# One matmul for both token halves: reversing the second half of the tokens in an HGRN2 recurrence

## The chip, the cores and the metric

The kernel runs on one core of a Trainium2 chip. The metric is the device time of one execution, in microseconds (us). Five engines work at once: TensorE (PE; its weight loads are shown as PEld), VectorE (DVE), ScalarE (ACT), GpSimd (POOL) and SyncE (SP), which here only issues DMAs. A profile is of one execution.

## The reference, cut to what matters

Two transformer blocks over 256 tokens of 2048 features, all in fp32. The change concerns one part of the first block, a gated linear recurrence with 8 heads of 128 by 128, taken along the tokens:

```python
log_f = log(lb + (1 - lb) * sigmoid(z)); k = (1 - lb) * sigmoid(-z); qf = silu(q) * 128 ** -0.5
b = cumsum(log_f)                       # along the tokens
# for every token t, over all s <= t:
scores[t, s] = sum_k q[t, k] * k[s, k] * exp(b[t, k] - b[s, k])
o[t] = sum_s scores[t, s] * v[s]
```

The rest of the model depends on the order of the tokens too, in three places: rotary angles and the sliding window of the first block's attention, the rotary angles of the second block's attention, and a Fourier transform along the tokens.

## The kernel before, in words

The program's main queue is a list of weight blocks (`plan`, line 85): each block is 256 tokens by 512 columns of some projection, cut into units of 256 weight rows. A unit is two times two times three fp32r matmuls of 512 columns, since each factor is split into a high and a low part (`unit`, line 900). ScalarE copies the high part of a weight tile (`high`, line 1293) and VectorE subtracts it to get the low part (`low`, line 1862); the four `raw` places, and more places in the arena in some stretches, are loaded by DMAs on SP's queue in the order of `ITEMS` (line 659).

Everything else is woven between the units by hand. `timetable` (line 372) gives each stage the slot at which it starts, and `drive` (line 635) lets every live stage take one step for each slot, on each engine's own queue: a `yield` is a step to the next slot. Engines meet through semaphores (`e.wait_ge`).

The recurrence is such a stage, `hgrn(b)`, for b = 0, 1, a group of four heads each; b = 1 starts two slots after b = 0. `QT`, `KT` and `BT` hold q, k and b with the features on the partitions and 256 token columns a head, the two halves of 128 (m = 0, 1) side by side. The scores of a token in the second half against one in the first half are "level 0" (L = 128). Within each half of 128, seven levels (L = 64 to 1) split every run of 2L tokens in two: the earlier L tokens are keys and the later L are queries, and the reference point of the decay is the last of the earlier ones, so that no exponent is positive. For a level,

1. VectorE writes two tensor_tensors of 512 elements into `E` (the differences of b), ScalarE takes `exp` of all 1024, and VectorE multiplies by k and q in place (lines 2083 to 2089);
2. TensorE multiplies. At level 0 these are four matmuls, one a head, with 128 columns (line 1042). At the others eight, one a head and half: the stationary operand is the 128 columns of `E` of that half, keys and queries alike, and the moving operand is the 64 query columns, taken in runs of L (line 1050);
3. VectorE copies the scores that count from PSUM into `s` with a mask (`copy_predicated`, lines 2102 to 2106), one instruction a level.

Four matmuls for the diagonal follow a group of two heads at a time (line 1059), then the products with v (line 1071). On TensorE a level is one slot in four, and each group of four heads has its own; the levels of b = 0 and b = 1 alternate.

`copy` and `f` on ScalarE (line 1281), `tt` on VectorE (line 1837) and `mm` on TensorE (line 864) are helpers, so that the profile shows their line for all their callers.

Of the kernel before, what the change touches and what calls it, by code (L numbers as in the profile page):

```python
# [15 lines left out]
P = 128  # L16
# [14 lines left out]
K_ID, K_U, K_ONE, K_AM, K_HM = 0, 128, 256, 384, 640  # L31
K_IF = K_HM + 64 * len(LEVELS)
K_MH = K_IF + 32
K_N = K_MH + 4


def constants():
    c = np.zeros((P, K_N), np.float32)
    i, j = np.arange(P)[:, None], np.arange(P)[None, :]
    c[:, K_ID:K_ID + P] = i == j  # L40
    c[:, K_U:K_U + P] = i <= j
    c[:, K_ONE:K_ONE + P] = 1.0
    c[:, K_AM:K_AM + P] = np.where(j > i, 0.0, -1e30)
    c[:, K_AM + P:K_AM + 2 * P] = np.where(j <= i, 0.0, -1e30)
# [8 lines left out]
    ang = 2.0 * np.pi * ((t[:, None] * t[None, :]) % 256) / 256.0  # L53
# [428 lines left out]
def program(nc, A, out):  # L482
    es = ExitStack()
    with es:
# [79 lines left out]
        QT, KT, BT = (kb(o, 8).rearrange("p (h t) -> p h t", h=8) for o in (0, 8, 16))  # L564
# [42 lines left out]
        def hg_s(b):  # L607
            return kb(72 + 4 * b, 4).rearrange("p (h m t) -> p h m t", h=4, m=2)
# [240 lines left out]
        def pe(e):  # L849
# [159 lines left out]
            def hf(b):  # L1009
                yield from range(5)  # L1010
                e.wait_ge(*S.a_hf.at(b, "ln"))
                for s in range(2):
                    bk = bank(("hf", b, "c", s), S.v_hf, b, "c", s)
                    for z in range(2):
                        for m in range(2):
                            t = mm(bk[:, z * 256 + m * P:z * 256 + (m + 1) * P],
                                   TA[:, m, (2 * s + z) * P:(2 * s + z + 1) * P], CST[:, K_U:K_U + P], True, True)
# [14 lines left out]
            def hgrn(b):  # L1032
                E, s, x = hg_e(b), hg_s(b), hg_x(b)
                for n, L in enumerate((128,) + LEVELS):
                    yield
                    yield
                    yield
                    e.wait_ge(*S.v_hgrn.at(b, n, "m"))
                    if n == 0:
                        bk = bank(("hg", b, n), S.a_hgrn, b, "x")  # L1040
                        for h in range(4):
                            t = mm(bk[:, h * P:(h + 1) * P], E[:, h * 256:h * 256 + P], E[:, h * 256 + P:(h + 1) * 256], True, True)
                    else:
# [9 lines left out]
                k_, q_ = KT[:, 4 * b:4 * b + 4, :], QT[:, 4 * b:4 * b + 4, :]  # L1053
                for g in range(2):
                    bk = bank(("hgd", b, g), S.v_hgrn, b, "d", g)
                    for h in range(2):
                        for m in range(2):
                            ms = slice(m * P, (m + 1) * P)
                            t = mm(bk[:, (h * 2 + m) * P:(h * 2 + m + 1) * P], k_[:, 2 * g + h, ms], q_[:, 2 * g + h, ms], True, True)
                    t.then_inc(*S.p_hgrn.up(b, "d", g))  # L1060
# [6 lines left out]
                for m in range(2):  # L1067
                    bk = bank(("hgo", b, m), S.a_hgrn, b, "o", m)
                    for h in range(4):
                        o, vs = bk[:, h * P:(h + 1) * P], slice((4 * b + h) * P, (4 * b + h + 1) * P)  # L1070
                        t = mm(o, s[:, h, m, :], V[:, m, vs], True, m == 0)
# [200 lines left out]
        def act(e):  # L1272
# [128 lines left out]
            def hf(b):  # L1401
# [17 lines left out]
                for s in range(2):  # L1419
                    e.wait_ge(*S.p_hf.at(b, "k", s))  # L1420
                    e.wait_ge(*S.a_tab.at(1, 1))
                    e.wait_ge(*S.d_lbw.at())
                    copy(KT[:, 4 * b + 2 * s:4 * b + 2 * s + 2, :].rearrange("p s t -> p (s t)"),
                         BANK[bank_of["hf", b, "k", s]][:, :]).then_inc(*S.a_hf.up(b, "k", s))
                    yield

            def hq(b):
# [6 lines left out]
                for s in range(2):  # L1434
                    e.wait_ge(*S.p_hq.at(b, s))
                    copy(QT[:, 4 * b + 2 * s:4 * b + 2 * s + 2, :].rearrange("p s t -> p (s t)"),
                         BANK[bank_of["hq", b, s]][:, :], scale=float(128 ** -0.5)).then_inc(*S.a_hq.up(b, s))
# [232 lines left out]
            def fourier(l):  # L1670
                yield
                for g in range(8):
# [6 lines left out]
                    copy(cu[:, 0, 1, :], ps[:, 0, P:0:-1])  # L1679
                    copy(cu[:, 1, 1, :], ps[:, 1, P:0:-1], scale=-1.0).then_inc(*S.a_four.up(l, g))  # L1680
# [152 lines left out]
        def dve(e):  # L1833
# [150 lines left out]
            def att(half):  # L1984
                s, pt = att_s(half), att_p(half)
                mx, nm, e1, sm, rs = (att_stat(half, k) for k in range(5))
                for kvb in range(2):
                    h0 = 4 * (2 * kvb + half)
                    for n in range(2):
# [8 lines left out]
                        k0 = K_AM if n else K_AM + P  # L1998
# [47 lines left out]
            def hf(b):  # L2046
# [11 lines left out]
                for s in range(2):  # L2058
                    e.wait_ge(*S.p_hf.at(b, "c", s))
                    i.tensor_copy(BT[:, 4 * b + 2 * s:4 * b + 2 * s + 2, :].rearrange("p s t -> p (s t)"),  # L2060
                                  BANK[bank_of["hf", b, "c", s]][:, :]).then_inc(*S.v_hf.up(b, "c", s))
                    yield

            def hgrn(b):
                E, s, x = hg_e(b), hg_s(b), hg_x(b)
                q_, k_, b_ = (z[:, 4 * b:4 * b + 4, :] for z in (QT, KT, BT))
# [4 lines left out]
                for n, L in enumerate((128,) + LEVELS):  # L2071
                    nb = 256 // (2 * L) * 4

                    def cut(z):
                        w = z.rearrange("p h t -> p (h t)").rearrange("p (n z l) -> p n z l", z=2, l=L)
                        return w[:, :, 0, :], w[:, :, 1, :]
                    ev = E.rearrange("p (n z l) -> p n z l", z=2, l=L)
                    el, er = ev[:, :, 0, :], ev[:, :, 1, :]
                    (bl, br), (ql, qr), (kl, kr) = cut(b_), cut(q_), cut(k_)
                    ref = bl[:, :, L - 1:L].to_broadcast([P, nb, L])  # L2080
                    if n:
                        e.wait_ge(*S.p_hgrn.at(b, n - 1))
                    tt(el, ref, bl, ALU.subtract)
                    z = i.tensor_copy(er, br) if L == 128 else tt(er, br, ref, ALU.subtract)
# [7 lines left out]
                    if n:  # L2092
# [3 lines left out]
                        so = s.rearrange("p h m t -> p (h m) t").rearrange("p g (n z l) -> p g n z l", z=2, l=L)  # L2096
                        mk = CST[:, K_HM + 64 * (n - 1):K_HM + 64 * n].bitcast(I32).rearrange("p (n l) -> p n l", l=L)
                        ps = BANK[bank_of["hg", b, n]][:, :].rearrange("p (g n l) -> p g n l", g=8, l=L)
# [11 lines left out]
                for g in range(2):  # L2110
                    e.wait_ge(*S.p_hgrn.at(b, "d", g))
                    i.copy_predicated(s[:, 2 * g:2 * g + 2, :, :].rearrange("p h m t -> p (h m) t"),
                                      IDN.bitcast(I32).unsqueeze(1).to_broadcast([P, 4, P]),
                                      BANK[bank_of["hgd", b, g]][:, :].rearrange("p (g t) -> p g t", g=4)).then_inc(*S.v_hgrn.up(b, "d", g))
                yield from range(5)
                O, sq = E.rearrange("p (m n) -> p m n", m=2), s.rearrange("p h m t -> p (h m t)")
# [455 lines left out]
```

## Time and profile before

| | us |
|---|---|
| median of three runs | 2276.31 (2273.92 to 2279.29) |
| profiled execution, its own time | 2276.56 |
| its span, first to last instruction | 2274.8 |
| TensorE busy in the span | 2231.7 (98%) |
| VectorE busy | 1508.9 (66%) |
| ScalarE busy | 1114.3 (49%) |
| GpSimd busy | 43.6 (2%) |

TensorE's granted clock is 0.997 of full speed in the mean. Busy shares are averages over all stages, and a busy TensorE counts overlapping matmuls as one stretch, so that the distance from one start to the next tells more than a matmul's duration.

### The profile page before, as it was taken

Reading aid. Unit: us, or ns where it says so; the run is one execution under the profiler, and the core shown is the slowest. Engines: PE = TensorE matmul, PEld = TensorE weight load, DVE = VectorE, ACT = ScalarE, POOL = GpSimd, SP = SyncE. Lnnn points to the kernel's source line nnn. Section 1 sums busy time; section 2 is a strip of 40 time slices with the busy share of each in tenths; the row PEclk is TensorE's granted clock in tenths of the full one; section 3 lists DMA queues with packets and bytes.
Section 4 is the critical chain, followed back from the end, with each engine's and each line's share of the span. In section 5 each row is a group of like instructions: output and inputs, shape, how many; then the busy total and the mean of one; then the engine's idle time right before and its main releaser. Section 6 shows DMA issues by size and latency. Waiting matters only on the chain.

```text
span 2274.8 us, 27239 instructions
## 1 busy us (share of the span) xinstructions
PE 2231.7 (98%) x10708; PEld 1863.6 (82%) x10708; DVE 1508.9 (66%) x1887; ACT 1114.3 (49%) x1546; POOL 43.6 (2%) x64
## 2 busy tenths in 40 slices
PE   9999999999999999999999999999999999999997
PEld 7788888888887888888888888787898887788886
DVE  6575467768877777777777778766355566545655
ACT  6475455444445444444443444565466454446552
POOL 1000000100000000000000000000000000000000
PEclk9999999999999999999999999999999999999999
DMA  7544654499796888888889888473454583555573
GB/s 263 170 131 126 190 173 146 131 342 318 250 330 232 296 289 297 304 302 292 296 299 304 296 292 297 153 239 93 139 173 146 160 271 90 164 149 158 149 234 117
DMA packets 233263, 500.65 MB, mean 220 GB/s; under 512 B 15872, under 2 KB 24992, under 8 KB 231984
## 3 DMA queue, kind: packets, MB, share of 16 engines
q1 hardware_dynamic: 229872, 484.11, 65.9%
q0 software_dynamic: 3264, 14.81, 1.8%
q8 instruction: 84, 1.38, 0.2%
q14 instruction: 43, 0.35, 0.0%
HBM read 496.74 MB, written 2.12 MB: 219 GB/s over the span
## 4 chain that ended last, share of the span: by engine, by line
PE 89%; DVE 5%; ACT 3%; issue 1%; DMA 1%; POOL 0%; SPq 0%; POOLq 0%; ACTq 0%; DVEq 0%
PE bank L864 86%; PE bank L867 3%; DVE wl L1837 2%; ACT wh L1281 1%; ACT arena L1281 1%; DMA raw<-in_w_in 1%; DVE arena L1844 1%; DVE arena L1840 1%; DVE arena L1837 1%; DVE arena L1845 0%; DMA raw<-in_w_ple_gate 0%; ACT hh L1281 0%; DVE hl L1837 0%; DVE al L1837 0%; ACT L1281 0%
## 5 line engine op out<-in xcount | busy, mean ns | idle before, releaser
L1281 ACT ACTIVATE wh<-raw 128x1024 fp32r<-128x1024 f32 (+2 forms) x493 | 512.6, 1042 | 665.6 <-PE bank L864 623.1
L1837 DVE TENSOR_TENSOR wl<-raw,wh 128x1024 fp32r<-128x1024 f32 (+2 forms) x493 | 590.6, 1200 | 331.8 <-ACT wh L1281 329.4
L864 PE MATMUL bank<-wh,hh 128*128 128x512 f32 (+1 forms) x1568 | 620.8, 397 | 11.6 <-DVE hl L1837 7.0
L864 PE MATMUL bank<-wh,hl 128*128 128x512 f32 (+1 forms) x1568 | 606.1, 387 | 0.0
L864 PE MATMUL bank<-wl,hh 128*128 128x512 f32 (+1 forms) x1568 | 604.7, 387 | 0.0
L864 PE MATMUL bank<-wh,ah 128*128 128x512 f32 (+1 forms) x1168 | 457.3, 392 | 4.3 <-ACT arena L1281 2.6
L864 PE MATMUL bank<-wh,al 128*128 128x512 f32 (+1 forms) x1168 | 451.1, 387 | 0.0
L864 PE MATMUL bank<-wl,ah 128*128 128x512 f32 (+1 forms) x1168 | 450.2, 386 | 0.0
L864 PEld LDWEIGHTS bank<-wh,hh 128*128 128x128 f32 x1568 | 294.6, 188 | 71.3 <-issue 12.2
L1281 ACT ACTIVATE wh<-arena 128x1024 fp32r<-128x1024 f32 x191 | 202.5, 1061 | 295.4 <-PE bank L864 292.0
L864 PEld LDWEIGHTS bank<-wh,hl 128*128 128x128 f32 x1568 | 294.6, 188 | 61.0
L864 PEld LDWEIGHTS bank<-wl,hh 128*128 128x128 f32 x1568 | 295.2, 188 | 55.3
L1837 DVE TENSOR_TENSOR wl<-arena,wh 128x1024 fp32r<-128x1024 f32 x191 | 233.4, 1223 | 97.6 <-ACT wh L1281 96.1
L864 PEld LDWEIGHTS bank<-wh,ah 128*128 128x128 f32 x1168 | 219.2, 188 | 47.0 <-ACT arena L1281 3.4
L864 PEld LDWEIGHTS bank<-wh,al 128*128 128x128 f32 x1168 | 219.2, 188 | 44.2
L864 PEld LDWEIGHTS bank<-wl,ah 128*128 128x128 f32 x1168 | 219.5, 188 | 41.5
L864 PE MATMUL bank<-arena 128*128 128x128 f32 (+6 forms) x944 | 148.2, 304 | 2.0 <-DVE arena L1837 2.0
L864 PEld LDWEIGHTS bank<-arena 128*128 128x128 f32 (+1 forms) x944 | 130.2, 191 | 16.1 <-issue 4.8
L1844 DVE SCALAR_TENSOR_TENSOR arena<-arena,cols 128x1024 f32<-128x1024 f32 x101 | 129.1, 1278 | 0.0
L867 PE MATMUL bank<-cst,arena 128*128 128x128 f32 (+1 forms) x752 | 112.1, 275 | 8.8 <-DVE arena L1837 3.1
L867 PEld LDWEIGHTS bank<-cst,arena 128*128 128x128 f32 (+1 forms) x752 | 91.9, 141 | 33.1 <-ACT arena L1281 4.7
L1837 DVE TENSOR_TENSOR arena<-arena 128x512 f32<-128x512 f32 (+6 forms) x192 | 95.5, 541 | 24.2 <-ACT arena L1281 23.5
(126 smaller groups left out, 1397.5 us busy)
## 6 DMA issues: line engine op xcount, KB each, us to landing
raw<-in_w_in SPq DMA_DIRECT2D x247, 512.0 KB, 3.8
arena<-in_w_ada SPq DMA_DIRECT2D x106, 512.0 KB, 5.1
arena<-in_w_gate_up SPq DMA_DIRECT2D x100, 512.0 KB, 5.2
raw<-in_w_ada SPq DMA_DIRECT2D x86, 512.0 KB, 4.9
raw<-in_w_out SPq DMA_DIRECT2D x77, 512.0 KB, 4.8
raw<-in_w_gate_up SPq DMA_DIRECT2D x76, 512.0 KB, 5.2
arena<-in_w_down SPq DMA_DIRECT2D x47, 512.0 KB, 5.5
raw<-in_w_down SPq DMA_DIRECT2D x41, 512.0 KB, 5.6
```

Of the source, the lines that this page charges most:

```text
L864: return i.matmul(o, l, x, start=start, stop=stop, skip_group_check=False)
L867: return i.transpose(o, x, idn)
L1281: return i.activation(o, x, fn, scale=scale, **k)
L1837: return i.tensor_tensor(o, a, b, op)
L1840: return i.tensor_scalar(o, a, s1, s2, op0) if op1 is None else i.tensor_scalar(o, a, s1, s2, op0, op1)
L1844: return i.scalar_tensor_tensor(out=o, in0=a, scalar=s, in1=b, op0=op0, op1=op1)
```

## The change

The tokens of the second half are kept in reverse order: token 255 is the first of that half and 128 the last (`TOKENS`). The inputs that run along the tokens are reordered outside the program, and the result is put back. Inside, the cumulative sum of that half uses a triangular matrix of the other side, the attention masks and the Fourier table are written for the new order, and the Fourier copies read forward.

In each run of 2L positions, the earlier tokens are now the first L positions in the first half and the last L in the second half. So the key positions of the two halves complement each other: for each head and level, the 64 key columns of the one half and the 64 of the other are gathered into 128 contiguous columns of `E`, and the 128 query columns into another 128. One matmul of 128 by 128 a head then holds the scores of both halves, each half in its own rows and columns; what would mix the halves is not copied. The masked copy of a level becomes two instructions, one for each half, with a mask that has one column for each run. `QT`, `KT`, `BT` and `s` are laid out with the half ahead of the head. The diff, cut:

```diff
+TOKENS = [*range(128), *range(255, 127, -1)]
...
+    c[:, K_U + P:K_U + 2 * P] = i >= j
...
     for n, L in enumerate(LEVELS):
-        for b in range(P // (2 * L)):
-            o = K_HM + 64 * n + b * L
-            c[2 * L * b:2 * L * b + L, o:o + L] = 1.0
+        for m in range(2):
+            for b in range(64 // L):
+                r = 2 * L * b + m * L
+                c[r:r + L, K_LV[n] + m * (64 // L) + b] = 1.0
...
-        QT, KT, BT = (kb(o, 8).rearrange("p (h t) -> p h t", h=8) for o in (0, 8, 16))
+        QT, KT, BT = (kb(o, 8).rearrange("p (b m h t) -> p b m h t", b=2, m=2, h=4) for o in (0, 8, 16))
...
+        def hg_at(off, m_step, L, l_size):
+            return bass.AP(tensor=AR[:, :].tensor, offset=off, ap=[[88 * 256, P], [m_step, 2], [2 * L, 256 // L], [1, l_size]])
+
+        def hg_cut(k, L):
+
+            o = 256 * k
+            return hg_at(o, 512 + L, L, L), hg_at(o + L, 512 - L, L, L), hg_at(o + L - 1, 513, L, 1)
...
                     e.wait_ge(*S.v_hgrn.at(b, n, "m"))
-                    if n == 0:
-                        bk = bank(("hg", b, n), S.a_hgrn, b, "x")
-                        for h in range(4):
-                            t = mm(bk[:, h * P:(h + 1) * P], E[:, h * 256:h * 256 + P], E[:, h * 256 + P:(h + 1) * 256], True, True)
-                    else:
-                        bk = bank(("hg", b, n), S.v_hgrn, b, n, "p")
-                        for h in range(4):
-                            for m in range(2):
-                                c0 = h * 256 + m * P
-                                rhs = E[:, c0:c0 + P].rearrange("p (n z l) -> p n z l", z=2, l=L)[:, :, 1, :]
-                                o = bk[:, (2 * h + m) * 64:(2 * h + m + 1) * 64].rearrange("p (n l) -> p n l", l=L)
-                                t = mm(o, E[:, c0:c0 + P], rhs, True, True)
+                    bk = bank(("hg", b, n), S.v_hgrn, b, n, "p") if n else bank(("hg", b, n), S.a_hgrn, b, "x")
+                    for h in range(4):
+                        t = mm(bk[:, h * P:(h + 1) * P], E[:, h * P:(h + 1) * P], E[:, 512 + h * P:512 + (h + 1) * P], True, True)
                     t.then_inc(*S.p_hgrn.up(b, n))
...
-                    copy(KT[:, 4 * b + 2 * s:4 * b + 2 * s + 2, :].rearrange("p s t -> p (s t)"),
-                         BANK[bank_of["hf", b, "k", s]][:, :]).then_inc(*S.a_hf.up(b, "k", s))
+                    copy(KT[:, b, :, 2 * s:2 * s + 2, :],
+                         BANK[bank_of["hf", b, "k", s]][:, :].rearrange("p (h m t) -> p m h t", h=2, m=2)).then_inc(*S.a_hf.up(b, "k", s))
...
-                    copy(cu[:, 0, 1, :], ps[:, 0, P:0:-1])
-                    copy(cu[:, 1, 1, :], ps[:, 1, P:0:-1], scale=-1.0).then_inc(*S.a_four.up(l, g))
+                    copy(cu[:, 0, 1, :], ps[:, 0, 1:P + 1])
+                    copy(cu[:, 1, 1, :], ps[:, 1, 1:P + 1], scale=-1.0).then_inc(*S.a_four.up(l, g))
...
                     if n:
                         e.wait_ge(*S.p_hgrn.at(b, n - 1))
+                        (_, qr, _), (kl, _, _), (bl, br, ref) = (hg_cut(k + 4 * b, L) for k in (0, 8, 16))
+                        el, er = (E[:, 512 * z:512 * z + 512].rearrange("p (g m l) -> p m g l", m=2, l=L) for z in range(2))
+                        ref = ref.to_broadcast([P, 2, 256 // L, L])
...
-                        if nn == 1:
-                            z = i.copy_predicated(so[:, :, 0, 1, :], mk.to_broadcast([P, 8, L]), ps[:, :, 0, :])
-                        elif L == 1:
-                            z = i.copy_predicated(so[:, :, :, 1, 0], mk[:, :, 0].unsqueeze(1).to_broadcast([P, 8, nn]), ps[:, :, :, 0])
-                        else:
-                            z = i.copy_predicated(so[:, :, :, 1, :], mk.unsqueeze(1).to_broadcast([P, 8, nn, L]), ps)
+                        for m in range(2):
+                            o = K_LV[n - 1] + m * nn
+                            mk = CST[:, o:o + nn].bitcast(I32)
+                            so = s[:, m].rearrange("p h (n z l) -> p h n z l", z=2, l=L)[:, :, :, 1 - m, :]
+                            ps = BANK[bank_of["hg", b, n]][:, :].rearrange("p (h n m l) -> p h n m l", h=4, m=2, l=L)[:, :, :, m, :]
+                            if nn == 1:
+                                z = i.copy_predicated(so[:, :, 0, :], mk.unsqueeze(2).to_broadcast([P, 4, L]), ps[:, :, 0, :])
+                            elif L == 1:
+                                z = i.copy_predicated(so[:, :, :, 0], mk.unsqueeze(1).to_broadcast([P, 4, nn]), ps[:, :, :, 0])
+                            else:
+                                z = i.copy_predicated(so, mk.unsqueeze(1).unsqueeze(3).to_broadcast([P, 4, nn, L]), ps)
                         z.then_inc(*S.v_hgrn.up(b, n, "p"))
```

The copies of q (ScalarE) and of the cumulative sum (VectorE) change as that of k does, and the diagonal's masked copy follows the new order of `s`. The constants go from 1124 to 1058 columns.

## Rows read from the trace of the kernel before

**Rows 1.** The chain that ended last, from the page: shares of the span by engine.
```profile
PE 89%; DVE 5%; ACT 3%; issue 1%; DMA 1%; POOL 0%; SPq 0%; POOLq 0%; ACTq 0%; DVEq 0%
```

**Rows 2.** Windows: stretch, its length, busy us of each engine, clock, DMA share, GB/s.
```profile
100.00:200.00 100.00, 99.49 (x531) 82.85 (x529) 63.85 (x106) 68.07 (x128) 0.00 (x0) 1.00 0.46 135
...
320.00:340.00 20.00, 20.00 (x110) 17.22 (x108) 14.23 (x18) 12.63 (x14) 0.00 (x0) 1.00 0.48 154
...
400.00:420.00 20.00, 20.00 (x113) 17.37 (x112) 17.12 (x21) 9.75 (x10) 0.00 (x0) 1.00 0.44 130
```

**Rows 3.** TensorE's waits, 300 to 500 us, then 100 to 300: us, times, longest.
```profile
PE bank L864 <- DVE wl L1837: 0.5, 1, 0.5
...
PE bank L867 <- ACT arena L1281: 0.5, 1, 0.5
```

**Rows 4.** Groups by form, 315 to 440 us: busy us, mean ns | idle before.
```profile
L1837 DVE TENSOR_TENSOR arena<-arena 128x512 f32<-128x512 f32 x56 | 36.0, 684 | 2.8 <-ACT arena L1281 2.8
...
L864 PE MATMUL bank<-arena 128*128 128x64 f32 x224 | 26.5, 271 | 0.0
...
L864 PE MATMUL bank<-arena 128*128 128x128 f32 x72 | 9.0, 274 | 0.0
```

**Rows 5.** Timeline of TensorE: first and last of fourteen level groups, and the next unit.
```profile
324.71 1.89 PE L864 MATMUL bank<-arena 128*128 128x64 f32 x16
326.42 0.48 PE L864 MATMUL bank<-wh,hh 128*128 128x512 f32 x1
...
420.94 1.89 PE L864 MATMUL bank<-arena 128*128 128x64 f32 x16
422.64 0.48 PE L864 MATMUL bank<-wh,hh 128*128 128x512 f32 x1
```

**Rows 6.** Timeline of TensorE: a level-0 group and a diagonal, with what follows.
```profile
318.37 1.05 PE L864 MATMUL bank<-arena 128*128 128x128 f32 x8
319.18 0.48 PE L864 MATMUL bank<-wh,hh 128*128 128x512 f32 x1
...
416.42 1.95 PE L864 MATMUL bank<-arena 128*128 128x128 f32 x16
418.12 0.48 PE L864 MATMUL bank<-wh,hh 128*128 128x512 f32 x1
```

**Rows 7.** Timeline of VectorE over one pair of upper levels, idle before in brackets.
```profile
326.64 0.74 DVE L2102 COPY_PREDICATED arena<-cst,bank 128x512 f32<-128x512 int32 x1 [2.07 <-PE bank L864]
...
332.99 1.29 DVE L1837 TENSOR_TENSOR arena<-arena 128x512 f32<-128x512 f32 x2 [0.96 <-ACT arena L1281]
...
337.89 1.23 DVE L1837 TENSOR_TENSOR wl<-raw,wh 128x1024 fp32r<-128x1024 f32 x1 [0.65 <-ACT wh L1281]
341.19 0.74 DVE L2106 COPY_PREDICATED arena<-cst,bank 128x512 f32<-128x512 int32 x1 [2.07 <-PE bank L864]
```

**Rows 8.** The same over the two lowest levels.
```profile
399.25 1.32 DVE L2106 COPY_PREDICATED arena<-cst,bank 128x512 f32<-128x512 int32 x1 [2.08 <-PE bank L864]
...
410.50 1.23 DVE L1837 TENSOR_TENSOR wl<-raw,wh 128x1024 fp32r<-128x1024 f32 x1 [0.42 <-ACT wh L1281]
413.79 1.32 DVE L2104 COPY_PREDICATED arena<-cst,bank 128x512 f32<-128x512 int32 x1 [2.07 <-PE bank L864]
414.91 1.31 DVE L1837 TENSOR_TENSOR arena<-arena 128x512 f32<-128x512 f32 x2
```

**Rows 9.** Groups of VectorE by form, whole execution: tensor_tensors of 256 elements.
```profile
L1837 DVE TENSOR_TENSOR arena<-arena 128x256 f32<-128x256 f32 x8 | 3.0, 418 | 0.0
```

**Rows 10.** Groups by form, whole execution: VectorE's and ScalarE's evictions.
```profile
L2060 DVE COPY arena<-bank 128x512 f32<-128x512 f32 x4 | 2.8, 689 | 2.1 <-PE bank L864 2.1
...
L1281 ACT ACTIVATE arena<-bank 128x512 f32<-128x512 f32 x107 | 60.2, 594 | 30.1 <-PE bank L867 22.6 <-PE bank L864 7.3
...
L1281 ACT ACTIVATE arena<-bank 128x128 f32<-128x128 f32 x32 | 7.0, 276 | 0.0
```

**Rows 11.** A piece of the chain that ended last, in order of time: start, us, what.
```profile
469.87 12.02 DMA raw<-in_w_in
```

More of the change, by code:

```diff
@@ L29 @@
 SCL = float(192 ** -0.5)
-K_ID, K_U, K_ONE, K_AM, K_HM = 0, 128, 256, 384, 640
-K_IF = K_HM + 64 * len(LEVELS)
+K_ID, K_U, K_AM, K_HM = 0, 128, 384, 768
+K_LV = [K_HM + sum(128 // v for v in LEVELS[:n]) for n in range(len(LEVELS) + 1)]
+K_IF = K_LV[-1]
 K_MH = K_IF + 32
 K_N = K_MH + 4
+TOKENS = [*range(128), *range(255, 127, -1)]
 def constants():
@@ L41, in constants @@
     c[:, K_U:K_U + P] = i <= j
-    c[:, K_ONE:K_ONE + P] = 1.0
-    c[:, K_AM:K_AM + P] = np.where(j > i, 0.0, -1e30)
-    c[:, K_AM + P:K_AM + 2 * P] = np.where(j <= i, 0.0, -1e30)
+    c[:, K_U + P:K_U + 2 * P] = i >= j
+    c[:, K_AM:K_AM + P] = np.where(j > 127 - i, 0.0, -1e30)
+    c[:, K_AM + P:K_AM + 2 * P] = np.where(j >= i, 0.0, -1e30)
+    c[:, K_AM + 2 * P:K_AM + 3 * P] = np.where(j <= i, 0.0, -1e30)
     for n, L in enumerate(LEVELS):
-        for b in range(P // (2 * L)):
-            o = K_HM + 64 * n + b * L
-            c[2 * L * b:2 * L * b + L, o:o + L] = 1.0
+        for m in range(2):
+            for b in range(64 // L):
+                r = 2 * L * b + m * L
+                c[r:r + L, K_LV[n] + m * (64 // L) + b] = 1.0
     half = 32
@@ L52, in constants @@
     t = np.arange(256)
-    ang = 2.0 * np.pi * ((t[:, None] * t[None, :]) % 256) / 256.0
+    ang = 2.0 * np.pi * ((np.array(TOKENS)[:, None] * t[None, :]) % 256) / 256.0
     sc = 1.0 / np.sqrt(256.0 * 128.0)
@@ L1070, in hgrn @@
                         o, vs = bk[:, h * P:(h + 1) * P], slice((4 * b + h) * P, (4 * b + h + 1) * P)
-                        t = mm(o, s[:, h, m, :], V[:, m, vs], True, m == 0)
+                        t = mm(o, s[:, m, h, :], V[:, m, vs], True, m == 0)
                         if m == 1:
@@ L1435, in hq @@
                     e.wait_ge(*S.p_hq.at(b, s))
-                    copy(QT[:, 4 * b + 2 * s:4 * b + 2 * s + 2, :].rearrange("p s t -> p (s t)"),
-                         BANK[bank_of["hq", b, s]][:, :], scale=float(128 ** -0.5)).then_inc(*S.a_hq.up(b, s))
+                    copy(QT[:, b, :, 2 * s:2 * s + 2, :],
+                         BANK[bank_of["hq", b, s]][:, :].rearrange("p (h m t) -> p m h t", h=2, m=2), scale=float(128 ** -0.5)).then_inc(*S.a_hq.up(b, s))
                     yield
@@ L1997, in att @@
                             e.wait_ge(*S.p_op.at("H1", 7))
-                        k0 = K_AM if n else K_AM + P
+                        k0 = K_AM if n else K_AM + 2 * P
                         mask = CST[:, k0:k0 + nk].unsqueeze(1).to_broadcast([P, per, nk])
@@ L2059, in hf @@
                     e.wait_ge(*S.p_hf.at(b, "c", s))
-                    i.tensor_copy(BT[:, 4 * b + 2 * s:4 * b + 2 * s + 2, :].rearrange("p s t -> p (s t)"),
-                                  BANK[bank_of["hf", b, "c", s]][:, :]).then_inc(*S.v_hf.up(b, "c", s))
+                    i.tensor_copy(BT[:, b, :, 2 * s:2 * s + 2, :],
+                                  BANK[bank_of["hf", b, "c", s]][:, :].rearrange("p (h m t) -> p m h t", h=2, m=2)).then_inc(*S.v_hf.up(b, "c", s))
                     yield
@@ L2065, in hgrn @@
                 E, s, x = hg_e(b), hg_s(b), hg_x(b)
-                q_, k_, b_ = (z[:, 4 * b:4 * b + 4, :] for z in (QT, KT, BT))
                 e.wait_ge(*S.a_hq.at(b, 1))
@@ L2071, in hgrn @@
                 for n, L in enumerate((128,) + LEVELS):
[L2072 to L2080, printed above, removed]
                     if n:
                         e.wait_ge(*S.p_hgrn.at(b, n - 1))
+                        (_, qr, _), (kl, _, _), (bl, br, ref) = (hg_cut(k + 4 * b, L) for k in (0, 8, 16))
+                        el, er = (E[:, 512 * z:512 * z + 512].rearrange("p (g m l) -> p m g l", m=2, l=L) for z in range(2))
+                        ref = ref.to_broadcast([P, 2, 256 // L, L])
+                    else:
+                        bl, br = BT[:, b, 0], BT[:, b, 1]
+                        el, er = (E[:, 512 * m:512 * m + 512].rearrange("p (h t) -> p h t", h=4) for m in range(2))
+                        kl, qr, ref = KT[:, b, 0], QT[:, b, 1], bl[:, :, P - 1:P].to_broadcast([P, 4, P])
                     tt(el, ref, bl, ALU.subtract)
-                    z = i.tensor_copy(er, br) if L == 128 else tt(er, br, ref, ALU.subtract)
+                    z = tt(er, br, ref, ALU.subtract) if n else i.tensor_copy(er, br)
                     z.then_inc(*S.v_hgrn.up(b, n, "s"))
@@ L2095, in hgrn @@
                         nn = 64 // L
-                        so = s.rearrange("p h m t -> p (h m) t").rearrange("p g (n z l) -> p g n z l", z=2, l=L)
-                        mk = CST[:, K_HM + 64 * (n - 1):K_HM + 64 * n].bitcast(I32).rearrange("p (n l) -> p n l", l=L)
-                        ps = BANK[bank_of["hg", b, n]][:, :].rearrange("p (g n l) -> p g n l", g=8, l=L)
                         if n > 1:
                             e.wait_ge(*S.v_hgrn.at(b, n - 1, "p"))
-                        if nn == 1:
-                            z = i.copy_predicated(so[:, :, 0, 1, :], mk.to_broadcast([P, 8, L]), ps[:, :, 0, :])
-                        elif L == 1:
-                            z = i.copy_predicated(so[:, :, :, 1, 0], mk[:, :, 0].unsqueeze(1).to_broadcast([P, 8, nn]), ps[:, :, :, 0])
-                        else:
-                            z = i.copy_predicated(so[:, :, :, 1, :], mk.unsqueeze(1).to_broadcast([P, 8, nn, L]), ps)
+                        for m in range(2):
[7 more added lines that the diff above has]
+                                z = i.copy_predicated(so[:, :, :, 0], mk.unsqueeze(1).to_broadcast([P, 4, nn]), ps[:, :, :, 0])
+                            else:
+                                z = i.copy_predicated(so, mk.unsqueeze(1).unsqueeze(3).to_broadcast([P, 4, nn, L]), ps)
                         z.then_inc(*S.v_hgrn.up(b, n, "p"))
@@ L2111, in hgrn @@
                     e.wait_ge(*S.p_hgrn.at(b, "d", g))
[L2112 to L2114 removed]
+                    i.copy_predicated(s[:, :, 2 * g:2 * g + 2, :], IDN.bitcast(I32).unsqueeze(1).unsqueeze(1).to_broadcast([P, 2, 2, P]),
+                                      BANK[bank_of["hgd", b, g]][:, :].rearrange("p (m h t) -> p m h t", m=2, h=2)).then_inc(*S.v_hgrn.up(b, "d", g))
                 yield from range(5)
[L2116 removed]
+                O, sq = E.rearrange("p (m n) -> p m n", m=2), s.rearrange("p m h t -> p (m h t)")
                 ss, r = hg_stat(b, 0), hg_stat(b, 1)
@@ L2562 @@
     data = {n: np.ascontiguousarray(inputs[n]) for n in _INS}
+    for n, axis in (("x", 1), ("p", 2), ("positions", 1), ("positions_2", 1)):
+        data[n] = np.ascontiguousarray(np.take(data[n], TOKENS, axis))
     data["k_cst"], data["k_cs"], data["k_cc"] = constants()
@@ L2570 @@
     program(nc, aps, o)
-    return run(nc, [arrays], core_ids=[0]).results[0]["out_0"]
+    return np.ascontiguousarray(run(nc, [arrays], core_ids=[0]).results[0]["out_0"][:, TOKENS])
```

9 lines of the change are left out of this document (4 added, 5 removed).

## The prediction

> **What bounds the kernel now.** I read the chain that ended last first: 89% of it lies on TensorE [rows 1]. What shortens TensorE's queue shortens the kernel, as long as nothing else ends later in its place. Then I looked for the stretch that the change touches: the recurrence's levels, whose matmuls are woven between the column blocks of the gates. The windows show TensorE busy there for 20.00 of 20 us at full clock, VectorE for 14.23 at the start and 17.12 where the last levels run [rows 2]. The waits say the same from the other side: from 300 to 500 us TensorE waits once, 0.5 us, for a weight split and not for the recurrence [rows 3]. So the stretch is a solid TensorE queue, and VectorE is the second engine, near enough to be watched. Last I read the groups by form for what the recurrence costs on each engine [rows 4], and the timelines of TensorE and VectorE for how the pieces follow one another [rows 5 to 8].
>
> The reader should see one oddity. Every fp32 matmul of the recurrence leaves two records, and a record of 64 columns is as long as one of 128, 271 against 274 ns [rows 4]. The queue tells it better than these durations, which overlap: eight matmuls of 128x64 (16 records) hold it from 324.71 to 326.42, 1.71 us [rows 5]; four of 128x128 (8 records) from 318.37 to 319.18, 0.81 us; eight of 128x128, the diagonal's, from 416.42 to 418.12, 1.70 us [rows 6]. What counts is how many matmuls there are, about 0.21 us each, and not how wide they are up to 128.
>
> **The change, part by part.**
>
> *Level matmuls.* Each of seven levels, for each of two groups of four heads, issues eight matmuls of 128x64 today: 14 groups, 112 matmuls, the 224 records of rows 4. After it, four of 128x128 with both operands contiguous: the form, layout and count of the level-0 group, which the trace times. Saved for each group: 1.70 − 0.81 = 0.89 us (1.70 again in the last of the fourteen, 420.94 to 422.64). 14 × 0.89 = 12.5 us. Bounds: if the new form paced at the diagonal's rate, 1.70/2 = 0.85, the saving is 11.9; the highest is 14 × (1.71 − 0.81) = 12.6.
>
> The Trainium skill, page "TensorE: Matmul & The Clock Gate", section "Back-to-back issue gap", speaks against this: a warm matmul follows the one before after N/2.4 + 2.5 ns, so that eight of 64 columns and four of 128 take nearly the same time and nothing is saved. Rows 5 and 6 contradict it here (16 records of half the width take twice as long as 8). The same page's section "LDWEIGHTS (loading the stationary operand)" gives 128/1.2 = 107 ns for a load whatever the moving width is; by it, an estimate, 112 loads fewer are 12.0 us.
>
> *Predicated copies.* The 14 copies of the levels' scores on VectorE each become two of half the size, since the halves that are kept lie differently for the two token halves. One takes 0.74 us at an upper level and 1.32 at the two lowest, with runs of two elements and of one [rows 7, 8]. A 256-element tensor_tensor takes 418 ns against 684 for 512 [rows 4, 9], so halving drops 0.27, and a second instruction adds 0.47 − 0.27 = 0.20 us; neighbours overlap in the queue by some 0.05 to 0.1 (two tensor_tensors of 0.68 last 1.29 in rows 7), so about 0.15 a level. At the lowest two each half takes 1.32 − 0.53 = 0.79, some 0.25 more for both. I take 10 × 0.15 + 4 × 0.25 = 2.5 us on VectorE over the stretch. The trace does not show such a copy with a mask that repeats within a run, nor one that reads PSUM in steps. Below, two halves run like one and the extra is 0. Above, I let a level's two copies cost twice today's one, a little over the ratio between the dearest and the cheapest of rows 7 and 8: +0.74 at the upper levels, +1.32 at the lowest.
>
> Is that covered? VectorE's pair of levels (one of each head group) runs from 326.64 to 341.19, 14.55 us, of which it idles 0.96 + 0.65 + 2.07 = 3.68, the last being its wait for TensorE's group [rows 7]: 10.87 us of work. TensorE's pair shrinks by 2 × 0.89 to 12.77, and 10.87 + 0.30 fits. At the lowest levels the pair 399.25 to 413.79 idles 0.42 + 2.07, so 12.05 of work [rows 8]; with 0.5 more, 12.55 against 12.76. It just fits. If not, there is a cushion: the products that the last group waits for are ready at 414.91 + 1.31 = 416.22, and the group starts at 420.94: 4.7 us early [rows 5, 8]. Behind the copies in VectorE's queue stand the other group's products and the weight splits, which TensorE needs. The upper bound gives 10.87 + 1.48 = 12.35 a pair, still within 12.77, and 12.05 + 2.64 = 14.69 in the two lowest pairs: a lag of 1.9 each, 3.8 in all, under the cushion. Hence nothing in the sum, and up to 2 us in the range, since the cushion is read at one group.
>
> *Differences and products.* The same 56 tensor_tensors of 512 elements [rows 4], on patterns with one dimension more. Two of them last 1.29 us at an upper level and 1.31 at the lowest, where they step by two elements [rows 7, 8]: short runs are free as far as the trace shows. I take no change. Bound above: double per element, +0.53 each; this is rival C.
>
> *Evictions in a new order.* Four copies each of k, q and the cumulative sum (8 on ScalarE, 4 on VectorE) write the same 512 elements with two dimensions swapped [rows 10]. From 100 to 300 us TensorE stood still once, for 0.5 us [rows 3]; doubled, the twelve would add some 7 us to two engines that are busy for 64 and 68 of 100 us there [rows 2]. Taken at nothing; without that cover, at most the 7 us. The diagonal's four copies keep their size. The Fourier copies (32 of 128x128, 276 ns) read forward in place of backward: off the chain, at nothing too.
>
> *Nothing moves in a queue.* No DMA, wait or slot is moved; the load of the constants gets 66 columns narrower. The tokens are reordered outside the program.
>
> *Where time could be lost again.* Everything behind the recurrence comes 12 us earlier, by the same slots. The place to watch is 469.87, where the chain passes through a weight load of 12.02 us [rows 11] in a queue that also waits for the recurrence's end. It is released by the same splits as before, so it shifts along; TensorE's only wait there is 0.5 us now [rows 3].
>
> **Sum.** The profiled execution took 2276.56 us (span 2274.8, 1.8 around it), 0.25 above the median of the three runs. 2276.6 − 12.5 = 2264.1: 2264 us, −0.55%.
>
> **Rivals.**
> A. *VectorE becomes the pace in part.* The copies cost more than the upper bound, or ScalarE's exponentials come late for a VectorE that has no idle left, and some of the gain goes into waits for products or splits. At twice the lag of the bound, 7.6 us, 2.9 come back behind the cushion of 4.7, and all 7.6 without it: 2267 to 2272. For it: 17.12 of 20 us busy. Against: the cushion. 8%.
> B. *No gain.* The array is paced by columns, which stay as many; then 2276.5. The 0.21 us for either width speaks against it; for it, only that the level-0 form is timed in few groups. 5%.
> C. *Slower.* The longer patterns of the differences and products cost double per element: 8 × 0.53 = 4.2 us in each pair on VectorE, 10.87 + 0.30 + 4.2 = 15.4 against today's 14.55. Seven pairs lag 6 us behind today's pace, the lowest two add 2 × 1.4 (12.05 + 0.5 + 4.2 = 16.8), less 4.7 of cushion: some 2281. It decides from 14.55 − 10.87 = 3.7 us extra a pair, that is 0.46 on each of eight instructions. The Trainium skill, page "SBUF — State Buffer", section "Door 1: The DMA port swizzle", says that each access into a new 16-byte line pays a penalty, with lines of 8 bytes in PSUM, which speaks for such a price; the lowest level's products in rows 8 do not bear it out, the 1.32 us of the lowest copies may. 4%.
> Forecast: 83%.
>
> **How the numbers follow.** Three runs lie 2.4 below to 3.0 above their median; below about 0.2% (4.6 us) a difference can't be told from none. The forecast's own range is 2261 to 2268 (11.9 to 12.6 saved, 2 us of VectorE's bound, the spread). Most of A takes the upper end to 2270; B, C and the rest of A stay out: 2260 to 2270. Faster by over 0.2% (below 2271.7): the forecast and most of A, 0.90. Same: B and a little of A, 0.06. Slower: C, 0.04.
>
> **What would show it.** Fourteen level groups of 8 records of 128x128, each holding TensorE's queue 0.8 us. No gap on TensorE from 320 to 430 us, and the last level group some 11.6 us (13 shorter groups before it) nearer to the level-0 group. VectorE's wait before the first head group's copy falling from 2.07 us to nearly nothing, its copies now 28, of about 0.47 and 0.79 us, the products as long as before. Wrong would be: TensorE waits on VectorE between level groups (A, C), records of 128x128 spaced 0.2 us (B), or a wait much over 0.5 us near 470.

## The result, and the profile after

The changed kernel takes 2263.68 us (median of four runs, 2263.41 to 2266.70) against 2277.22 for the kernel before on the same chip (2273.92 to 2279.29): a ratio of 0.9945, 95% interval 0.9928 to 0.9962. It is faster by 0.55%, and 2264 had been predicted. The profiled execution took 2263.44 us, 13.1 less than that of before.

The page of the changed kernel: engines (busy us, share of the span, instructions), and further down the shares of the chain that ended last.

```profile
PE 2221.3 (98%) x10596; PEld 1853.6 (82%) x10596; DVE 1509.7 (67%) x1901; ACT 1114.9 (49%) x1546; POOL 43.6 (2%) x64
...
PE 90%; DVE 5%; ACT 3%; issue 1%; DMA 1%; POOL 0%; SPq 0%; POOLq 0%; ACTq 0%; DVEq 0%
```

The bound is where it was [rows 1]: 98% of the span busy, 90% of the chain. TensorE has less to do, and nothing has taken its place. What was line 864 is now line 881, 1281 is 1288 and 1837 is 1844. Its groups by form, 315 to 425 us, show the 128x64 records [rows 4] gone:

```profile
L1844 DVE TENSOR_TENSOR arena<-arena 128x512 f32<-128x512 f32 x58 | 37.5, 688 | 2.5 <-ACT arena L1288 2.5
...
L881 PE MATMUL bank<-arena 128*128 128x128 f32 x181 | 23.4, 274 | 0.0
...
L2112 DVE COPY_PREDICATED arena<-cst,bank 128x256 f32<-128x256 int32 x20 | 8.8, 499 | 5.5 <-PE bank L881 5.5
...
L2110 DVE COPY_PREDICATED arena<-cst,bank 128x256 f32<-128x256 int32 x4 | 2.6, 755 | 2.7 <-PE bank L881 2.7
...
L2108 DVE COPY_PREDICATED arena<-cst,bank 128x256 f32<-128x256 int32 x4 | 1.5, 441 | 1.2 <-PE bank L881 1.2
```

The timeline of TensorE: the level-0 group of b = 1, the first, the second and the last of the fourteen level groups, all but the second with the unit matmul behind it.

```profile
320.85 1.05 PE L881 MATMUL bank<-arena 128*128 128x128 f32 x8
321.66 0.48 PE L881 MATMUL bank<-wh,hh 128*128 128x512 f32 x1
...
327.20 1.05 PE L881 MATMUL bank<-arena 128*128 128x128 f32 x8
328.01 0.48 PE L881 MATMUL bank<-wh,hh 128*128 128x512 f32 x1
...
333.55 1.05 PE L881 MATMUL bank<-arena 128*128 128x128 f32 x8
...
411.51 1.05 PE L881 MATMUL bank<-arena 128*128 128x128 f32 x8
412.31 0.48 PE L881 MATMUL bank<-wh,hh 128*128 128x512 f32 x1
```

A group now holds the queue 0.81 us, where it held it 1.71 [rows 5]. The same unit matmul gives the whole gain: behind level 0 it starts at 321.66 instead of 319.18 [rows 6], 2.48 later; behind the last level group at 412.31 instead of 422.64 [rows 5], 10.33 earlier. Over the fourteen groups that is 12.81 us, 0.915 each. The 2.48 us were lost far ahead of the recurrence, behind 63 us (last section).

VectorE over a pair of upper levels, and over the two lowest (idle before, in brackets):

```profile
328.29 0.78 DVE L2108 COPY_PREDICATED arena<-cst,bank 128x256 f32<-128x256 int32 x2 [1.23 <-PE bank L881]
328.96 1.29 DVE L1844 TENSOR_TENSOR arena<-arena 128x512 f32<-128x512 f32 x2
...
334.55 1.29 DVE L1844 TENSOR_TENSOR arena<-arena 128x512 f32<-128x512 f32 x2 [0.82 <-ACT arena L1288]
335.76 0.77 DVE L2108 COPY_PREDICATED arena<-cst,bank 128x256 f32<-128x256 int32 x2
...
340.98 0.77 DVE L2112 COPY_PREDICATED arena<-cst,bank 128x256 f32<-128x256 int32 x2 [1.00 <-PE bank L881]
...
391.76 1.32 DVE L2112 COPY_PREDICATED arena<-cst,bank 128x256 f32<-128x256 int32 x2 [1.00 <-PE bank L881]
392.87 1.31 DVE L1844 TENSOR_TENSOR arena<-arena 128x512 f32<-128x512 f32 x2
...
404.45 1.32 DVE L2110 COPY_PREDICATED arena<-cst,bank 128x256 f32<-128x256 int32 x2 [0.89 <-PE bank L881]
405.56 1.32 DVE L1844 TENSOR_TENSOR arena<-arena 128x512 f32<-128x512 f32 x2
```

Both halves of a level's copy together last 0.77 us at an upper level, against 0.74 for the one instruction of before [rows 7], and 1.32 at the lowest two, as long as one [rows 8]. The pair from 328.29 to 340.98 lasts 12.69 us and idles 0.82 + 1.00: 10.87 us of work, the figure of before. VectorE still waits 0.9 to 1.2 us for the first head group's matmuls. From 300 to 500 us TensorE waits for nobody in this execution: the list of its waits there is empty. Near 470, the place to watch, the piece of 12.02 us through a weight load [rows 11] has left the chain, which runs on in TensorE's own queue (the second profile of the same kernel, e0_changed below, differs in this):

```profile
454.30 25.70 PE bank L881 x112
```

Windows of the stretch (stretch, length, busy us of PE, PEld, DVE, ACT and POOL, clock, DMA share, GB/s):

```profile
320.00:340.00 20.00, 20.00 (x102) 17.00 (x101) 16.43 (x23) 14.03 (x15) 0.00 (x0) 1.00 0.51 149
...
380.00:400.00 20.00, 20.00 (x102) 16.99 (x101) 18.17 (x27) 12.45 (x13) 0.00 (x0) 1.00 0.52 160
```

VectorE went from 14.23 [rows 2] to 16.43 of 20, since the same work now lies in fewer microseconds, and comes to 18.17 later. The question for the experiments: is it the count of matmuls that paid, and how near is VectorE to taking the gain back?

### The profile page after: what moved, and what is told of

Read it like the earlier page. It is cut to its first block, busy times and chain, and to the rows that moved or that the text cites. A ratio compares the mean times of both kernels' runs of the same rounds, so it can differ in the third digit from the quotient of the medians.

```text
span 2261.6 us, 27029 instructions
## 1 busy us (share of the span) xinstructions
PE 2221.3 (98%) x10596; PEld 1853.6 (82%) x10596; DVE 1509.7 (67%) x1901; ACT 1114.9 (49%) x1546; POOL 43.6 (2%) x64
## 4 chain that ended last, share of the span: by engine, by line
PE 90%; DVE 5%; ACT 3%; issue 1%; DMA 1%; POOL 0%; SPq 0%; POOLq 0%; ACTq 0%; DVEq 0%
PE bank L881 87%; PE bank L884 3%; DVE wl L1844 2%; ACT arena L1288 1%; ACT wh L1288 1%; DVE arena L1851 1%; DVE arena L1844 1%; DVE arena L1847 1%; DVE arena L1852 0%; ACT hh L1288 0%; DMA raw<-in_w_ple_gate 0%; DMA raw<-in_w_in 0%; DVE al L1844 0%; DVE hl L1844 0%; ACT L1288 0%
## 5 line engine op out<-in xcount | busy, mean ns | idle before, releaser
L881 PE MATMUL bank<-arena 128*128 128x128 f32 (+6 forms) x832 | 136.5, 309 | 2.0 <-DVE arena L1844 2.0
L881 PEld LDWEIGHTS bank<-arena 128*128 128x128 f32 (+1 forms) x832 | 117.7, 190 | 16.1 <-issue 4.8
```

The costliest lines, as they stand in the source:

```text
L881: return i.matmul(o, l, x, start=start, stop=stop, skip_group_check=False)
```

## The experiments

All start from the changed kernel. The kernel before, run beside them, had a median of 2276.2 us (first four kernels below) or 2276.3 (last three).

**Twice as many matmuls, half as wide** (e1_two64). Only the number of matmuls goes back: each of the four of a level becomes two of 64 columns with the same stationary operand. Layout, copies and results stay those of the change.

```diff
 for h in range(4):
-    t = mm(bk[:, h*P:(h+1)*P], E[:, h*P:(h+1)*P], E[:, 512+h*P:512+(h+1)*P], True, True)
+    for c in range(0, P, 64 if n else P):
+        w = 64 if n else P
+        o = h * P + c
+        t = mm(bk[:, o:o+w], E[:, h*P:(h+1)*P], E[:, 512+o:512+o+w], True, True)
```

> The changed kernel with one thing undone: each level's matmul of 128 columns is issued as two of 64, with the same weights loaded twice; layout, masks, copies and evictions stay as changed. Theory (the number of matmuls sets TensorE's time, 0.21 us each up to 128 columns): a level group holds TensorE 1.70 us again, 14 x 0.89 = 12.5 us come back, and the time is that of the kernel before, 2276 us within 3. Rival (the gain came from the layout, the contiguous operands or the lighter copies): the time stays at 2264. Rival (columns set the time): groups stay at 0.81 us and the time at 2264.

Measured: 2276.39 us (2274.81 to 2279.24), ratio 1.0002 (0.9992 to 1.0011). All of the gain is gone. Groups by form, then the first level group in the timeline of TensorE:

```profile
L881 PE MATMUL bank<-arena 128*128 128x64 f32 x224 | 26.5, 271 | 0.0
...
325.54 1.89 PE L881 MATMUL bank<-arena 128*128 128x64 f32 x16
327.24 0.48 PE L881 MATMUL bank<-wh,hh 128*128 128x512 f32 x1
```

The group holds the queue 1.70 us again, and nothing else of the change was undone. The total columns are as many as with four of 128, so the columns don't set the time. The moving columns are contiguous here and lay in runs of L in the kernel before, whose groups held the queue 1.71 us [rows 5]: the runs cost nothing that shows.

**As many matmuls, half as wide** (e2_four64). The kernel leaves out the scores of the second 64 columns.

```diff
-    t = mm(bk[:, h*P:(h+1)*P], E[:, h*P:(h+1)*P], E[:, 512+h*P:512+(h+1)*P], True, True)
+    o, w = h * P, 64 if n else P
+    t = mm(bk[:, o:o+w], E[:, h*P:(h+1)*P], E[:, 512+o:512+o+w], True, True)
```

> The changed kernel, whose four level matmuls stream only the first 64 of the 128 query columns; the scores of the other half of the columns are left out. Theory (count): a group of four still holds TensorE about 0.8 us, and the time stays at 2264 within 3. Rival (columns): a group takes 0.4 us, and 14 x 0.4 = 5.6 us go, to 2258.

Measured: 2263.7 us (2263.14 to 2264.27), ratio 0.9944 (0.9924 to 0.9964), the time of the changed kernel. Its timeline of TensorE, the first level group:

```profile
325.86 1.00 PE L881 MATMUL bank<-arena 128*128 128x64 f32 x8
326.67 0.48 PE L881 MATMUL bank<-wh,hh 128*128 128x512 f32 x1
```

Half the columns, and the same 0.81 us. From 64 to 128 columns the width costs nothing that shows.

**Half as many matmuls, twice as wide** (e3_two256). Two of 256 columns a level in place of four of 128. Half of what they compute are products of one head with another's, and the scores of two heads are left out.

```diff
-    for h in range(4):
-        t = mm(bk[:, h*P:(h+1)*P], E[:, h*P:(h+1)*P], E[:, 512+h*P:512+(h+1)*P], True, True)
+    for h in range(2 if n else 4):
+        w = 256 if n else P
+        t = mm(bk[:, h*w:(h+1)*w], E[:, h*P:(h+1)*P], E[:, 512+h*w:512+(h+1)*w], True, True)
```

> The changed kernel, whose levels issue two matmuls of 256 columns in place of four of 128: the same columns stream, but for two heads against the weights of one, so half the scores are of other heads. If the count set the time beyond 128 columns too, a group would take 0.42 us and 5.4 us would go, to 2258. If columns set it from 128 on (0.21 us for 128 in four passes of fp32 would then be the limit of both at once), a group stays at 0.8 to 0.85 us and the time at 2264 within 3. I expect the second.

Measured: 2264.09 us (2263.02 to 2265.15), ratio 0.9946 (0.9926 to 0.9966): no gain over the change. Timeline of TensorE, the first level group and the start of the next:

```profile
326.12 1.02 PE L881 MATMUL bank<-arena 128*128 128x256 f32 x4
326.79 0.58 PE L881 MATMUL bank<-wh,hh 128*128 128x512 f32 x1
327.21 0.40 PE L881 MATMUL bank<-wl,hh 128*128 128x512 f32 x1
...
332.47 1.02 PE L881 MATMUL bank<-arena 128*128 128x256 f32 x4
```

The next unit matmul starts 0.67 us after the group, but the one behind it only at 1.09, and the groups follow each other in 6.35 us, as in the changed kernel (327.20 to 333.55). Half the matmuls save nothing, so between 128 and 256 columns the width has begun to count, and merging beyond 128 does not pay here. In all these kernels each matmul loads its weights anew, so the runs don't tell the price of a matmul from that of its weight load.

**More copies on VectorE** (e4_copies2, e4_copies3). Each level's two copies are issued twice, or three times. They write the same values, so only VectorE's time grows.

```diff
-for m in range(2):
-    ... one half's copy_predicated
+for rep in range(2):        # 3 in e4_copies3
+    for m in range(2):
+        ... one half's copy_predicated
+    if rep < 1:             # 2 in e4_copies3
+        then(z, S.v_rep, b, n, rep)
```

> The changed kernel with each level's two masked copies issued twice, one set behind the other: some 0.87 us more of VectorE for an upper level (0.77 and a pause between) and 1.4 for each of the lowest two, about 14 us in all. Theory (VectorE is hidden, with its idle of 1.8 us in a pair of levels of 12.7 and a cushion of over 4 us behind it): upper pairs 10.9 + 1.75 = 12.6 still fit, the lowest two lag by 1.9 each, under the cushion; the time stays at 2264 within 3, and TensorE shows no wait between the groups. Rival (VectorE paces the stretch): all 14 us show, 2278.

> The changed kernel with each level's two masked copies issued three times, one set behind the other. By the run with two sets, a further set costs VectorE 0.80 us at an upper level and 1.35 at the lowest two. Theory (VectorE counts only once it is full and the cushion is used up): an upper pair of levels needs 10.9 + 3.2 = 14.1 us against TensorE's 12.7, a lag of 1.4 in each of five; the lowest two pairs 11.8 + 5.4 = 17.2, a lag of 4.5 each; 16 us in all, less some 4.7 of cushion: 11 us come back, 2275 within 3, and TensorE waits on VectorE's products between groups. Rival (VectorE never reaches TensorE here): 2264.

Measured: two sets 2265.0 us (2264.06 to 2265.94), ratio 0.995 (0.993 to 0.997); three sets 2272.51 (2269.92 to 2273.71), ratio 0.9979 (0.9969 to 0.999). A window of the kernel with two sets:

```profile
360.00:380.00 20.00, 20.00 (x102) 17.00 (x101) 19.71 (x35) 10.60 (x11) 0.00 (x0) 1.00 0.59 166
```

VectorE is busy 19.71 of 20 us, and TensorE loses nothing: the list of its waits from 300 to 470 us is empty, and from the unit matmul behind level 0 to the one behind the last level group it takes 90.65 us (320.67 to 411.32), as in the changed kernel (321.66 to 412.31). With three sets, windows of the later levels:

```profile
380.00:400.00 20.00, 18.77 (x91) 15.20 (x90) 19.79 (x33) 12.70 (x13) 0.00 (x0) 1.00 0.53 153
400.00:420.00 20.00, 15.39 (x85) 13.12 (x86) 19.86 (x29) 9.41 (x10) 0.00 (x0) 1.00 0.36 110
```

Its waits of TensorE from 300 to 470 us (us in total, times, longest):

```profile
PE bank L881 <- DVE arena L1844: 7.7, 5, 2.5
```

And the longest of them in its timeline of TensorE:

```profile
402.29 1.16 PE L881 MATMUL bank<-arena 128*128 128x128 f32 x8 [2.54 <-DVE arena L1844]
```

This is rival A, made to happen: level groups wait for their products, and most of the gain goes. It begins between one and two extra sets, each some 0.80 us a level at the upper ones and 1.35 at the lowest two. The change itself added under 0.1 at the upper ones.

**Filling two waits, and the changed kernel again** (e5_keep, e0_changed). These concern the time that the profiled execution of the changed kernel lost behind 63 us. There, and near 1440 us, TensorE waits about 3 us for VectorE. The edit fills these two waits with transposes of constants whose results nobody reads.

```diff
 def q(b):
     yield from range(5)
+    if b == 0:
+        keep(26, "q")
     e.wait_ge(*S.v_rope.at("q", b, 1))
...
     f = slot("pproj", 0)
     ahead(f + 1, "close", "Y3", "")
...
+    ahead(f + 2, "keep", 24, "ple")
```

> The changed kernel with TensorE kept at work in two holes outside the change: 26 transposes of a constant before the wait at 60 us (3.1 us long) and 24 before the one at 1441 us (2.8 us), as the kernel already does elsewhere. In the profiles so far the granted clock falls to 0.50 to 0.7 behind the first hole in five of six and behind the second in three of six. Theory (what the clock loses there is what separates executions of one kernel): the clock stays at 1.00 behind both, 1 to 2.5 us go at the first and up to 1.3 at the second, and the time is 2261.5 within 1.5, some 2 us under the changed kernel of the same call. Rival (the holes' ends are set by VectorE and the fillers delay the next matmuls, or the clock there costs nothing on the chain): no difference.

> The changed kernel again, unaltered, beside the run that keeps TensorE at work, and to narrow its ratio to the kernel before: 2264 within 1.5, ratio 0.9945. If the gain is the level matmuls alone, the ratio is 0.9944 (12.8 us of the shift that the profile shows over the fourteen groups).

Measured: 2260.9 us filled (2259.84 to 2261.95), ratio 0.9932 (0.9918 to 0.9946); 2262.72 unfilled (2261.71 to 2263.35), ratio 0.9939 (0.9926 to 0.9952). The first place, filled, in the timeline of TensorE:

```profile
59.34 3.00 PE L885 MATMUL bank<-cst 128*128 128x128 f32 x26
...
62.60 0.66 PE L885 MATMUL bank<-cst,arena 128*128 128x128 f32 x4 [0.26 <-DVE arena L1847]
```

Its windows behind both waits:

```profile
64.00:68.00 4.00, 4.00 (x21) 3.29 (x20) 3.09 (x3) 2.99 (x6) 0.00 (x0) 1.00 1.04 390
1440.00:1444.00 4.00, 4.00 (x21) 3.32 (x20) 3.03 (x5) 2.02 (x5) 0.00 (x0) 1.00 0.43 131
```

The second of these windows in e0_changed, unfilled:

```profile
1440.00:1444.00 4.00, 4.00 (x14) 3.29 (x14) 3.03 (x5) 0.84 (x2) 0.00 (x0) 0.59 0.46 132
```

Filled, the clock stays at 1.00 behind both waits, and in the second window 21 matmuls run where 14 ran. Behind the first wait e0_changed shows 1.00 unfilled too (table in the last section), so that one profile proves little there; but over whole executions the mean granted clock is 0.998 in each of the five filled ones and 0.997 in each of the five unfilled. On the whole time, 1.8 us between the medians is under 0.1%, and the two intervals overlap: that filling is worth it is likely, and not settled.

The run e0_changed is also a second profile of the changed kernel. Its unit matmuls behind level 0 and behind the last level group in the timeline of TensorE, its only wait of TensorE from 300 to 500 us (us, times, longest), and a piece of its chain near 470:

```profile
318.68 0.48 PE L881 MATMUL bank<-wh,hh 128*128 128x512 f32 x1
...
409.33 0.48 PE L881 MATMUL bank<-wh,hh 128*128 128x512 f32 x1
...
PE bank L881 <- DVE wl L1844: 0.8, 1, 0.8
...
456.53 12.29 DMA raw<-in_w_in
```

Against the kernel before the first is 0.50 us earlier and the last 13.31: over the fourteen groups 12.81 us, as in the first profile. The wait for a weight split and the way of the chain through a weight load are there again.

## Why the prediction was right, point by point

*The time: right, and nearer than could be known.* 2264 was forecast, 2263.68 measured, and 2262.72 in e0_changed. The 95% interval of the ratio leaves the gain anywhere from 8.7 to 16.4 us, and the profiled executions differ by more than the level matmuls (last point), so that an agreement within half a microsecond is in part luck.

*Level matmuls: right, a little small.* Forecast 14 × 0.89 = 12.5 us, measured 12.81 in both profiles. The groups' own time came out as read (0.81 for 1.71); some 0.015 a group more lies in the units between them, and why is open. That the count of matmuls pays was only read from rows 5 and 6; e1 and e2 show it. They settle rival B too: it needed columns to pace the array, and e2 halves them for nothing. The gap rule that the Trainium skill gives ("TensorE: Matmul & The Clock Gate", section "Back-to-back issue gap"), taken as a rule for this stream, would have e1 and the change take nearly the same time; they differ by 12.7 us. That section of the Trainium skill itself notes that its formula counts too little at narrow widths, for want of the weight load, a remark that the prediction passed over. The Trainium skill's rule for a load, on the same page (section "LDWEIGHTS (loading the stationary operand)"), by an estimate 107 ns for 128 columns, is near the 106 ns at which e1's sixteen records follow one another (1.70 / 16). That the load sets this pace is not shown: the records of e1's weight loads last 191 ns each in the mean, and overlap.

*Copies: mis-sized, in the safe direction.* I took +0.15 us at an upper level and +0.25 at a lowest. From the copy's start to the next instruction's, an upper level's two halves take 0.67 us (328.29 to 328.96), and the one copy of before took 0.64 (326.64 [rows 7] to 327.28):

```profile
327.28 1.27 DVE L1837 TENSOR_TENSOR arena<-arena 128x512 f32<-128x512 f32 x2
```

At a lowest level both take some 1.1 (404.45 to 405.56; 413.79 to 414.91 [rows 8]). So 0.03 us was added at this upper level, and nothing at a lowest. The step that failed is the price of a second instruction behind the first. The halves by themselves came out near what I had worked out, 0.44 us (L2108) and 0.755 (L2110) against 0.47 and 0.79. But two of them overlap by more than the 0.05 that I had taken off at an upper level: 2 × 0.44 us lasts 0.78, an overlap of 0.10, and 2 × 0.755 lasts 1.32, an overlap of 0.19, where I had taken off none. Stepped reads of PSUM and the repeating mask cost nothing that shows. It changed no time, since VectorE had room.

*The cushion: right, and larger than said.* A whole extra set of copies, about the upper bound that I had put on them (+0.74 and +1.32), shows no cost (e4_copies2); a second one costs 9.8 us over the changed kernel run beside it (2272.51 − 2262.72). So rival A's mechanism is real, and its condition was not near. VectorE at nearly 99% of a window still delayed nobody.

*VectorE's wait before the copies: wrong in size.* It was to fall from 2.07 us to nearly nothing, and fell to 0.9 to 1.2. The pair did shrink, from 14.55 to 12.69, but VectorE's work did not grow by the 0.3 us that I had added, and of the 1.86 us of idle time that went, only 1.07 came out of this wait (2.07 to 1.00); the rest came out of those before the products and the split (0.96 + 0.65 to 0.82).

*Differences and products: right.* 688 ns against 684; rival C needed 460 ns more on each. The section of the Trainium skill that the prediction names for C ("SBUF — State Buffer", "Door 1: The DMA port swizzle") also calls strides of up to four fp32 elements free, which the prediction left out. The lowest level's products step by two, and come near it: two of them last 1.31 to 1.32 us, against 1.29 at an upper level.

*Evictions: right.* VectorE's copies of the cumulative sum take 690 ns in the mean against 689 [rows 10], and ScalarE's group that holds those of k and q 595 against 594; ScalarE's and VectorE's busy time over the whole page moved by less than 1 us, and TensorE's waits ahead of the recurrence are as before.

*Behind the recurrence: as said in one profile, better in the other.* In e0_changed the chain's detour through a weight load shifted along (456.53 for 469.87), with a wait of 0.8 us where there was one of 0.5 [rows 3]. In the first profile both are gone, some 0.6 us of gain that I had not counted. So this differs between executions of one kernel, and, with one profile of the kernel before, it can't be counted as a gain of the change. The first two profiled executions differ by 13.1 us: these 12.81 and 0.6, less 2.7 that the changed kernel lost to the clock behind 63 us, and 2.4 of other differences, of both signs, most of them far behind the recurrence. The clock fell in the kernel before near 1454 us (0.76 and 0.81 in the 4 us from 1452 and from 1456), and in the changed kernel near 1908 (0.57 in the 4 us from there); and a wait of TensorE near 1500 us lasts 1.48 us in the former and 0.30 in the latter.

## What to carry to other kernels

Read the price of a small fp32 matmul from the distance between starts in a packed queue, not from its duration, and look for the width below which it is flat; up to there, merging pairs into one pays by the matmul, even when half of each product is thrown away. Past it a merge buys nothing (here from 128 to 256 columns). Before counting the gain, ask how much more work the second engine can take before the first one waits; doubling that work on purpose measures it.

## What the runs showed of the hardware that was not expected

TensorE waits 3.1 us for VectorE near 60 us in both kernels. A window of 4 us behind that wait, of before:

```profile
64.00:68.00 4.00, 4.00 (x21) 3.29 (x20) 3.56 (x4) 3.02 (x5) 0.00 (x0) 1.00 1.03 379
```

The same window of the changed kernel, and the one in which the wait ends:

```profile
60.00:64.00 4.00, 1.11 (x5) 1.11 (x6) 3.86 (x10) 1.80 (x3) 0.00 (x0) 0.73 0.72 252
64.00:68.00 4.00, 4.00 (x11) 3.10 (x10) 3.38 (x3) 1.78 (x3) 0.00 (x0) 0.50 1.00 386
```

After the same wait, one execution stays at 1.00 of the clock (2.4 GHz) and runs 21 matmuls; the other falls to 0.50 (1.2 GHz) and runs 11. In the timelines of TensorE this reads as follows, the end of the wait and a unit matmul soon after, of before:

```profile
63.07 0.66 PE L867 MATMUL bank<-cst,arena 128*128 128x128 f32 x4 [3.10 <-DVE arena L1837]
...
66.67 0.48 PE L864 MATMUL bank<-wh,hh 128*128 128x512 f32 x1
```

The same two of the changed kernel:

```profile
62.89 1.11 PE L884 MATMUL bank<-cst,arena 128*128 128x128 f32 x4 [3.10 <-DVE arena L1844]
...
69.16 0.47 PE L881 MATMUL bank<-wh,hh 128*128 128x512 f32 x1
```

It comes out of the wait 0.18 us earlier and reaches the unit matmul 2.49 us later: the lower clock cost 2.7 us. The wait itself does not decide it. Behind it the granted clock of 64 to 68 us was as follows; a figure between the two levels is the mean of a window that holds both.

| profiled execution | clock, 64 to 68 us |
|---|---|
| before | 1.00 |
| changed | 0.50 |
| e1_two64 | 0.68 |
| e2_four64 | 0.59 |
| e3_two256 | 0.71 |
| e4_copies2 | 0.57 |
| e4_copies3 | 0.62 |
| e0_changed, the changed kernel again | 1.00 |
| e5_keep, wait filled | 1.00 |

The changed kernel shows both. So behind a wait of 3 us TensorE can run some microseconds at the lower clock, which cost up to some 2.7 us at this place. What decides within one execution was not found. Of the kernel before there is one profile alone, so whether the change makes such a fall likelier is open.
